# Adaptive-norm steps reordered, weights of the next stage split early, and a second latent layer that projects its index first

## The reference

```python
def layer_c(x, c, norm_mix, norm_ffn, mod_w, mod_b, w_in, w_out, wg, wu, wd):
    sh_m, sc_m, g_m, sh_f, sc_f, g_f = adaln(c, mod_w, mod_b)
    h = modulate(x, norm_mix, sh_m, sc_m)
    q, k, v, q_idx, k_idx, w_idx = _split_2(h @ w_in, IN1_SIZES)
    x = x + g_m[:, None, :] * (dsa_mixer(q, k, v, q_idx, k_idx, w_idx) @ w_out)
    h = modulate(x, norm_ffn, sh_f, sc_f)
    return x + g_f[:, None, :] * swiglu(h, wg, wu, wd)
...
        sc = jax.nn.relu(jnp.einsum('bqhd,bsd->bqhs', qi, k_idx) * IDX_DIM ** -0.5)
        idx_score = jnp.einsum('bqhs,bqh->bqs', sc, wi) * IDX_HEADS ** -0.5
        idx_score = jnp.where(kpos[None, :] <= tq[:, None], idx_score, -jnp.inf)
        _, sel = lax.top_k(idx_score, n_keep)
```

## Time and profile before

| | us |
|---|---|
| median of 3 runs | 2530.59 (2526.53 to 2533.37) |
| the profiled execution's own time | 2528.26 |
| its span | 2526.4 |
| PE busy | 2340.3 (93%) |
| VectorE busy | 1304.8 (52%) |
| ScalarE, GpSimd busy | 790.8, 337.8 |

### The profile page before, as it was taken

How to read it: one execution, slowest core, us unless ns; L and a number is a source line. 1 busy time by engine, 2 the same in 40 slices (tenths; PEclk the granted TensorE clock), 3 DMA queues, 4 the chain that set the end, 5 groups by cost and what they waited for, 6 DMA issues and landing times.

```text
span 2526.4 us, 30550 instructions
## 1 busy us (share of the span) xinstructions
PE 2340.3 (93%) x11882; PEld 1774.8 (70%) x11882; DVE 1304.8 (52%) x2847; ACT 790.8 (31%) x1671; POOL 337.8 (13%) x345
## 2 busy tenths in 40 slices
PE   7899999989999989979898989999988688999997
PEld 6766575578547566868765868888776467788876
DVE  4564746622454438365856266663437863433333
ACT  4154004411113017231447122223423361222233
POOL 2300100000100210020100110004521001000044
PEclk9999999989999999987979999999979899999999
DMA  7200330001240640033310135553213102222222
GB/s 288 92 18 18 125 117 34 2 16 63 92 150 1 156 147 3 32 119 126 118 34 2 67 124 176 184 188 128 93 66 118 51 1 67 100 97 89 99 100 75
DMA packets 58267, 225.89 MB, mean 89 GB/s; under 512 B 20478, under 2 KB 21118, under 8 KB 41740
## 3 DMA queue, kind: packets, MB, share of 16 engines
q1 hardware_dynamic: 58124, 223.94, 26.3%
HBM read 221.83 MB, written 2.10 MB: 89 GB/s over the span
## 4 chain that ended last, share of the span: by engine, by line
PE 77%; DVE 13%; DMA 3%; POOL 3%; ACT 2%; issue 2%; SPq 0%; POOLq 0%; DVEq 0%; ACTq 0%
PE PS L86 72%; PE PS L91 5%; DVE ACC L115 2%; DMA ADA<-in_l_mod 1%; DVE RINGr L103 1%; POOL WKr L103 1%; DVE WK L157 1%; DVE WK L108 1%; DVE WK L142 1%; DVE SM L152 1%; DVE WK L115 1%; DMA WK<-in_rpb 1%; ACT WK L98 1%; POOL Xr L103 1%; DVE WK L103 1%
## 5 line engine op out<-in xcount | busy, mean ns | idle before, releaser
L86 PE MATMUL PS<-Hr,GBr 128*128 128x512 f32 x1280 | 443.9, 400 | 25.7 <-DVE RINGr L103 20.4
L86 PE MATMUL PS<-Hr,RINGr 128*128 128x512 f32 x1040 | 406.5, 391 | 0.0
L96 ACT ACTIVATE WK<-PS 128x512 f32<-128x512 f32 (+3 forms) x390 | 189.8, 518 | 528.9 <-PE PS L86 326.7
L115 DVE SCALAR_TENSOR_TENSOR ACC<-ADA,SM,ACC 128x256 f32<-128x256 f32 x608 | 293.0, 505 | 91.5 <-DMA ACC<-in_l_mod_b 47.7
L86 PE MATMUL PS<-H,RING 128*128 128x512 f32 (+1 forms) x928 | 337.2, 515 | 0.0
L86 PEld LDWEIGHTS PS<-Hr,GBr 128*128 128x128 f32 x1280 | 243.8, 191 | 86.8 <-DVE RINGr L103 22.1
L103 DVE TENSOR_TENSOR RINGr<-RING,GBr 128x1024 fp32r<-128x1024 f32 (+1 forms) x155 | 199.3, 1324 | 165.5 <-ACT GBr L96 165.5
L86 PEld LDWEIGHTS PS<-H,RING 128*128 128x128 f32 x928 | 172.3, 191 | 135.0 <-issue 127.1
L86 PE MATMUL PS<-RING,GB 128*128 128x256 f32 x1156 | 252.8, 381 | 3.5 <-DVE GB L120 2.2
L86 PEld LDWEIGHTS PS<-RING,GB 128*128 128x128 f32 x1156 | 220.6, 191 | 34.4 <-issue 4.1
L86 PEld LDWEIGHTS PS<-Hr,RINGr 128*128 128x128 f32 x1040 | 199.2, 192 | 41.4
(11 more groups left out here) (192 smaller groups left out, 2933.9 us busy)
## 6 DMA issues: line engine op xcount, KB each, us to landing
ADA<-in_l_mod SPq DMA_DIRECT2D x96, 512.0 KB, 3.7
RING<-in_l_gu SPq DMA_DIRECT2D x44, 1024.0 KB, 4.9
RING<-in_l_wd SPq DMA_DIRECT2D x24, 1024.0 KB, 5.0
RING<-in_l_in SPq DMA_DIRECT2D x17, 1024.0 KB, 5.2
RING<-in_ev_in SPq DMA_DIRECT2D x13, 1024.0 KB, 5.8
ADA<-in_od_ada SPq DMA_DIRECT2D x24, 512.0 KB, 3.6
RING<-in_od_in SPq DMA_DIRECT2D x11, 1024.0 KB, 5.9
RING<-in_l_out SPq DMA_DIRECT2D x8, 1024.0 KB, 5.0
```

The lines of the kernel that those rows point to most:

```text
L86: self.last = self.eng.matmul(out, lhsT, rhs, start=start, stop=stop, skip_group_check=True)
L96: self.last = self.eng.activation(out, in_, func, bias=bias, scale=scale)
L115: self.last = self.eng.scalar_tensor_tensor(out=out, in0=a, scalar=s, in1=b, op0=op0, op1=op1)
```

## The change

The adaptive-norm groups get another order, and their calls move: out of the first latent layer's first projections and the second one's index projections, into the output projections of the even, odd and first latent layers; the feed-forward blocks take `ada(4)` in place of `ada(3)`. The first weight chunk of the next stage is split inside the last tile of the output projection before it, and `norm_mod` splits the second chunk instead. Odd low tiles of h go from POOL to DVE; so do activation tiles 40 and 41. The second latent layer's weights are cut anew: index keys with the index weights (`l1_ki`), index queries, keys with values, queries. Index scores are made by pairs of heads as the query products come, and `l1_q1` is projected beside the top-k.

```diff
+ADA_ORDER = (("ev", range(6)), ("od", range(4)), ("l0m", range(4)), ("od", (4, 5)), ("l0f", range(4)), ("l0m", (4, 5)),
+             ("l1m", range(4)), ("l0f", (4, 5)), ("l1f", range(4)), ("l1m", (4, 5)), ("l1f", (4, 5)))
...
     def hi_place(i, h, k, n):
+            elif name == "l1_ki":
+                place = GBr[:, 15360:15904] if h else EXQr[:, 0:544]
...
+        def hl_signal(st, k, gi):
+            return dve_value if (gi == 0 if wide(st) else k % 2) else pool_value
...
     tensor: ffn
-                    ada(3)
+                    ada(4)
     tensor: output projections of ev, od, l0
+                     lambda t: ada(4) if t < 4 else norm_mod("od", [(0, range(4))], by_h) if t == 4 else None)
+            out_proj("od_out", range(4), lambda k: None, lambda t: ada(3) if t < 3 else None)
+            out_proj("l0_out", range(4), lambda k: None, lambda t: ada(4) if t < 3 else None)
     tensor: l1m
-            tm_split("l1m", i, 0, 136, "vw", lambda t: [(dve_value, ("vw", t))])
-            fm_split("l1m", i, 0, "kk", 0, lambda s0: copied("kk", 0, s0))
-            fm_split("l1m", i, 1, "ki", 0, lambda s0: copied("ki", 0, s0))
-                    fm_split("l1m", i + 1 + j, m, "qi", t, lambda s0: copied("qi", t, s0))
-                    ada(3)
-            since(pe, "proj I")
+            fm_split("l1m", FIRST["l1_ki"], 0, "ki", 0, lambda s0: copied("ki", 0, s0))
+            weights_i(1)
+            queries_i(0)
+            weights_i(2)
+            queries_i(1)
+            weights_i(3)
+            chunk_done(FIRST["l1_ki"])
+            index_scores(0)
+            queries_i(2)
+            index_scores(1)
+            queries_i(3)
+            index_scores(2)
+            fm_split("l1m", i, 0, "kk", 0, lambda s0: copied("kk", 0, s0))
+            index_scores(3)
+            tm_split("l1m", i, 128, 128, "v1", lambda t: [(act_value, ("v1", t))])
...
     scalar: last tile of the output projection
                 norm_half("fin1", t, 0, "od_out")
+                if t == 3:
+                    round_chunk(FIRST["l0_in1"])
                 norm_half("fin1", t, 1, "od_out")
...
     vector: norm_mod
+                    if f > 1 and f % 2 == 0:
+                        lower(f - 1)
+                    elif f == 7:
+                        lower(7)
                     if f == 3 and st != "ev":
-                        rest({"l0m": FIRST["l0_in1"], "l0f": FIRST["l0_gu"], "l1m": FIRST["l1_vw"],
+                        rest({"l0m": FIRST["l0_in1"] + 1, "l0f": FIRST["l0_gu"] + 1, "l1m": FIRST["l1_ki"] + 1,
...
     vector: out_proj
                     for jj in range(2):
+                        if jj and t == tiles[-1] and nxt is not None:
+                            rest(FIRST[nxt])
                         add(name, st, t, jj, where["out", name, t, jj], cds[0] if t < 4 else cds[1], 2 * n + jj)
...
     gpsimd: lower
-                for f in range(8):
+                for f in range(8) if wide(st) else range(0, 8, 2):
...
     sync, after the odd layer's attention
-            sp.dma_start(GB[:, 15104:16128], brow(A["fin1"], 1024)).then_inc(fin_in["fin1"], "fin1", 16)
+            sp.dma_start(H[:, 0:1024], brow(A["fin1"], 1024)).then_inc(fin_in["fin1"], "fin1", 16)
+            for t in range(3):
+                ada(3)
             for j in range(4):
                 load()
...
     sync, after the first latent layer's attention
+            for t in range(3):
+                ada(4)
             for j in range(4):
                 load()
```

More of the change, by code:

```diff
@@ L221, in _ada_steps @@
     i = 0
-    for st, (w, c0, cds, g) in STAGES.items():
-        for grp in range(6):
+    for st, groups in ADA_ORDER:
+        w, c0, cds, g = STAGES[st]
+        for grp in groups:
             for j in range(2):
@@ L1390, in tensor, with weights_i @@
-            close(of_pe, "proj I")
-            since(pe, "proj I")
[L1392 to L1400, removed]
+            def weights_i(t):
+                tm_split("l1m", FIRST["l1_ki"], 128, 8, "wi", lambda t: [(dve_value, ("wi", t))], (t,))
@@ L1895, in scalar, with index_scores @@
             close(of_act, "norm l1m")
-            i = FIRST["l1_vw"]
+            since(act, "norm l1m")
+            def index_scores(t):
+                for n in range(1, 4):
+                    for h in range(2):
+                        z = t * 6 + n * 2 - 2 + h
+                        rl = WK[:, 2560 + z % 4 * 512:2560 + z % 4 * 512 + (n + 1) * 128]
+                        if z > 3:
+                            act.wait_ge(dve_value, ("idx", z - 4))
+                        act.wait_ge(pe_scores, ("idx", t, n, h))
+                        act.activation(rl, bank(where["idx", t, n, h], 0, (n + 1) * 128), ACT.Relu, scale=0.125)
+                        act.then_inc(act_value, ("idx", t, n, h))
@@ L2472, in twice @@
                 norm_tile("l0m", t)
-            out_proj("od_out", "od", range(4), ("c",), twice)
+                if t < 3:
+                    ada(3)
+            out_proj("od_out", "od", range(4), ("c",), twice, "l0_in1")
             cur.allowed |= {"l0f"}
@@ new lines, in index_scores @@
+            def index_scores(t):
+                for n in range(1, 4):
+                    w = (n + 1) * 128
+                    for h in range(2):
+                        z = t * 6 + n * 2 - 2 + h
+                        rl = WK[:, 2560 + z % 4 * 512:2560 + z % 4 * 512 + w]
+                        wc = Bg(wi + n * 8 + 2 * t + h, wi + n * 8 + 2 * t + h + 1)
+                        dve.wait_ge(act_value, ("idx", t, n, h))
+                        own(("wi", n))
+                        if t == 0 and h == 0:
+                            dve.tensor_scalar(SC(n), rl, wc, None, ALU.mult)
+                        else:
+                            own(last[n])
+                            dve.scalar_tensor_tensor(SC(n), rl, wc, SC(n), ALU.mult, ALU.add)
+                        last[n] = dve.then_inc(dve_value, ("idx", z))
@@ L2760, in ffn @@
                 for f in range(22):
-                    ada(3)
+                    ada(4)
                 ada_until(ADA_AFTER[st, 5])
-                for fz in range(42):
+                for fz in range(40):
                     own()
@@ L2889, in gpsimd @@
             since(pool, "norm l0m")
-            for t in range(8):
-                ada(2)
-            for j in range(2):
-                ada(2)
             for m in range(2):
@@ L3040, in sync @@
             ada_until(ADA_AFTER["od", 3])
+            for t in range(4):
+                ada(4)
             for j in range(4):
@@ L3067, in sync @@
             ada_until(ADA_AFTER["l0m", 3])
-            for j in range(4):
-                ada(2)
-                ada(2)
-                load()
-            for j in range(2):
-                load()
-                ada(2)
-            for j in range(2):
+            for j in range(8):
                 load()
@@ L3090, in sync @@
                 load()
-            for j in range(2):
-                ada(3)
-                ada(3)
-                load()
-            for j in range(4):
+            for j in range(6):
                 load()
```

218 lines of the change are left out of this document (106 added, 112 removed).

## The result

The changed kernel takes 2507.41 us (median of 4 runs, 2502.1 to 2510.09); the kernel before, on the same chip, 2530.73 (2526.53 to 2533.37). The ratio is 0.9909, 95% interval [0.9894, 0.9925]: 23.3 us faster. The forecast was 2520, 10.5 less than before. The sign is right and the time lies in the range, but the gain is more than twice the one forecast. The profiled execution has a span of 2504.3 for 2526.4, and the steps are checked against these 22.1 us.

A forecast was written before the change was run, and what follows sets the result against it. PE, busy 93% of the span, bounds the kernel, so stages are worth PE's waits. -30.2 - 2.4 + 7.0 + 5.3 - 11 - 3 - 1.6 + 18.7 + 5.7 + 1 = -10.5 us, giving 2520; range 2480 to 2541.

The forecast's parts named there:

- Feed-forward blocks (+18.7, +5.7): Gate groups with three chunk steps hold up rest; each PE wait costs 5.7 us: +18.7 first block, +5.7 last.
- 1.6 more where a fifth runs into the down projection: First feed-forward block: a fifth gate group reaching the down projection adds 1.6 us, inside the +18.7.
- Second latent layer (-30.2): Attention starts 30.2 us earlier, at 1966 for 1996.23, with PE and VectorE's top-k about level; ends -35 and -22.
- Seams where SP is late (+7.0, +5.3): Odd and first latent layers' output projections: weight loads queue behind ada, VectorE's last add is late: +7.0 and +5.3 us.
- Rival (2): SP gets through early at the two projections, seams give -2.4 each: 17 us more gain, 2503; chance 0.12.
- Low tiles on VectorE (-2.4 a seam): Four of a norm's low tiles on VectorE, four on GpSimd: last tile sooner, -2.4 us a seam (0 to -4).
- rival (4): At four seams each VectorE low tile waits for a GpSimd one of 1.5 us: +33, 2553 us; chance 0.04.
- First latent layer (-11, -12 at most): Its projections: all sums but two calls leave, so PE's waits and low clock go: -11 us (-6.6 to -12).
- Odd layer (-3): PE's wait of 3.33 us for a bias row goes, as the new order does not need it: -3 (-2 to -3.3).
- Activation tiles 40, 41 (-1.6): On VectorE they shorten the 2.33 us wait at each block's end: -1.6 us for two (0 to -7).
- Rival (1): Feed-forward blocks: third chunk step does not hold rest; -5.7 and 0 for +18.7 and +5.7, 2490 us; chance 0.14.
- Rivals (3) and (5): (3): plain groups stall too, 2544, chance 0.09; (5): low clock stays in second latent layer, gate waits 7 us, 2534, 0.11.

The follow-up runs named there:

- e1: Changed kernel with ada(3) again in place of ada(4) in both feed-forward blocks: 2494.57 us, ratio 0.9870 to the kernel before.
- the second trace: Trace of the changed kernel run again without any edit, as base for e1, e2 and e3: 2508.32 us, ratio 0.9922 to the kernel before.
- e9: Changed kernel with the edits of e1 and e3, and no ada call behind the 22nd chunk of a feed-forward block: 2481.96 us, ratio 0.9809.
- e5: Changed kernel with the second latent layer's index scores all behind the projections of keys and values: 2527.68 us, ratio 0.9995 to the kernel before.
- e6: Changed kernel with four ada(3) calls back between the second latent layer's query products, taken from the last feed-forward block: 2510.61 us, ratio 0.9931.
- e2: Changed kernel with SP's four weight loads ahead of the third ada call in the odd layer's output projection: 2501.52 us, ratio 0.9897.
- e3: Changed kernel with e2's edit, plus loads first and ada(3) for ada(4) in the first latent layer's output projection: 2494.43 us, ratio 0.9868.
- e7: Changed kernel with all eight low tiles of a norm on GpSimd again at four seams: 2516.67 us, ratio 0.9953 to the kernel before.

## Why the prediction was wrong in size

- **Feed-forward blocks (+18.7, +5.7): the step that failed.** The places, the cause and the number of waits were right (e1). The price was not: "From the chunk's end 1471.1 that is 14.9, and PE has 10.8 of other work: 4.0 of waiting, and 1.7 for the clock". It was copied from one occurrence. The term measured +7.9 from the end of the first block's second chunk on (+10.2 in the second trace), and +2.2 in the last block. Three things made it smaller: the third load took 3.5 us at all five groups and not 4.79 (the page of the profile gives 3.7 for either kernel as the median of the 96 loads); PE's own turning of the last sum filled 0.95; and behind the shorter waits the clock did not fall at four of the five (three of five in the second trace). The new wait of e9, where only the load is shorter, is 2.80, as this account has it. The sentence on the Trainium skill (DMA: Bandwidth & Descriptors, Anatomy of one DMA) gives an estimate of 3.2 us for 512 KB, by which the sum would have been 8 lower. The section's fit is for DMAs that GpSimd issues, and SP issues these; still it was nearer to the 3.46 to 3.56 measured here than the row I used. Why that one load took 4.79 is open.
- **"1.6 more where a fifth runs into the down projection".** A wait came there, 2.71 us, but from ScalarE's queue and not from a chunk step: it stood in e1 and went in e9.
- **Second latent layer (-30.2): right,** -31.4 (-28.1 in the second trace), PE and top-k level as said (PE's last product ends at 1976.4, attention starts at 1977.4). e5 and e6 put about 17 on the order and 8 to 9 on the sums; about 5 is not parted.
- **Seams where SP is late (+7.0, +5.3): right.** +9.0, and +4.5 up to the second chunk's end of the first block. VectorE's last add came 9.6 late at the first one, for the 9.4 of the working; the 2.4 set against it was not there. e2 shows the cause at the first seam and gives 6.8 back; e3 gives 7.1 back at the second, with shorter calls as well. Rival (2) is refuted.
- **Low tiles on VectorE (-2.4 a seam): right,** but for one seam: e7 puts it at 0 where the add is late and at 2.0 to 2.8 elsewhere; rival (4) is refuted. The rule of the Trainium skill (SBUF — State Buffer, Who interferes with whom), that the one engine waits for the other's whole instruction, is borne out in kind by the 1.32 us beside GpSimd for 0.68 alone. The loss that the prediction worked out from it did not come: e7 measured a gain.
- **First latent layer (-11, -12 at most):** its projections gained 14.5, but the stage behind them lost 3.8, with the same waits (3.60 and 3.08 for 3.95 and 3.11) and a mean granted clock of 0.86 for 0.87, some 2 us of the 3.8; an apply step that now stands at the stage's end (1384.77) is 0.8 more, and the rest is open.
- **Odd layer (-3):** not seen. The wait of 3.33 is gone, but PE waits 3.14 for 1.75 elsewhere. The next stage starts at 1020.2 to 1029.1 us in the twelve traces of the new order, in the middle at 1024.2, for 1022.5 before.
- **Activation tiles 40, 41 (-1.6):** the wait at each block's end is 1.80 us for 2.33. The down projections changed by +0.4 and -1.9, the first by -2.4 in the second trace, so the clock hides the term there.
- **Rival (1)** came half true: the third step holds `rest`, but for less than half of the time that I gave it. Rivals (3) and (5) did not come: no plain group made PE wait, and the second latent layer gained its 30 us.

## What to carry to other kernels

A wait is the difference of two long sums, so take each link from the median of its kind and add all work that the waiting engine has in between, before one occurrence is multiplied by five: 1.3 us of a load and 0.95 of matmuls turned 4.0 us into 1.7. When work is inserted ahead of the loads in the program of the engine that issues them, price what comes late behind them; here SP's order alone was worth 7 us at one seam. Removing a wait can be worth nothing when the work moves to a place where it makes another (e9). And before a stage is split into parts to a tenth of a microsecond, look at a second trace of the same kernel: here one stage differed by 3.3 us between two.

## What the runs showed of the hardware

- The length of a wait alone doesn't tell whether the clock falls behind it. The same kernel waited 2.71 us at the same place in two traces: the granted clock over the next 4 us was 0.57 in the one and 1.00 in the other. Behind 1.84 us at 1685.83 it was 0.62, behind 1.84 at 2161.66 it was 1.00. Where it fell at both ends of the first down projection, that stage took 128.7 us, and 125.9 where it did not; the next stage then took 121.9 and 125.2.
- The same instructions in the same order took PE to the odd layer's output projection at 1020.2 us in one trace (e3, the fastest execution of its run) and at 1029.1 in another (e9, the slowest of its run, on another chip); ten other traces of the new order lie between. A term of 3 us in that stage can't be read from one trace of each kernel.
